# Five mixing products placed in three parts of a streaming encoder layer on one core

## What is computed

```python
z = rms_norm(x, g_mix) @ w_in
q_lat, c_kv, k_r, u, v = split(z)
# group A: latent attention, 8 heads, for prompt and for sample
q = norm_rope(rms_norm(q_lat) @ w_q_up)
k, v_att = norm(c_kv_all @ w_kv_up)        # sample: 1024 cached rows + 64 new
o_att = softmax(q k / sqrt(96)) v_att
# group B: spatial gating, 8 groups of 64 columns, chunks of 128 positions
vn = layer_norm(gelu(v))
mixed = einsum('gij,bcjgd->bcigd', masked(w_s), vn) + b_s
o_gm = gelu(u) * mixed
x = x + concat(rms_norm(o_att), rms_norm(o_gm)) @ w_o
x = x + (silu(h @ w_gate) * (h @ w_up)) @ w_down     # h = rms_norm(x)
```

## Time and profile before

| | |
|---|---|
| median of 3 runs | 1410.85 us |
| lowest and highest | 1410.61 and 1413.23 us |
| time of the profiled execution | 1417.39 us |
| its span, first to last instruction | 1415.6 us |
| mean granted TensorE clock | 0.981 |
| PE busy | 1352.3 us (96%) |
| DVE, ACT, POOL busy | 912.7, 599.5, 866.3 us |

### The profile page before, as it was taken

One profiled execution on the slowest core, in us unless ns is written; L12 is line 12 of the kernel. 1 busy time (PEld: TensorE's weight loads), 2 busy tenths in 40 slices (PEclk: granted clock), 3 DMA queues, 4 the chain that ended last, 5 costly groups with the idle time before them and its releaser, 6 DMA issues.

```text
span 1415.6 us, 25340 instructions
## 1 busy us (share of the span) xinstructions
PE 1352.3 (96%) x9448; PEld 1247.7 (88%) x9448; DVE 912.7 (64%) x1490; ACT 599.5 (42%) x953; POOL 866.3 (61%) x460
## 2 busy tenths in 40 slices
PE   6999989998999999999999989889899999999998
PEld 6885657898999999999998756779899999999997
DVE  3456467487666766676736475665866766666665
ACT  4336467444333333333342365764443333333331
POOL 3645057286777777777655443464777777777771
PEclk8999999999999999999999999999999999999999
DMA  7110021131322222222421000221232222222221
GB/s 229 60 38 11 5 61 30 32 89 54 96 90 89 89 89 89 89 89 89 130 89 52 26 5 1 60 60 31 60 90 90 89 89 89 89 89 89 89 89 68
DMA packets 138577, 102.35 MB, mean 72 GB/s; under 512 B 8972, under 2 KB 125136, under 8 KB 138512
## 3 DMA queue, kind: packets, MB, share of 16 engines
q1 hardware_dynamic: 135848, 100.46, 23.6%
q10 hardware_dynamic: 2664, 1.02, 0.3%
HBM read 98.10 MB, written 3.36 MB: 72 GB/s over the span
## 4 chain that ended last, share of the span: by engine, by line
PE 83%; DVE 9%; ACT 2%; issue 2%; POOL 2%; DMA 1%; ACTq 0%; SPq 0%; DVEq 0%
PE ps L2199 33%; PE ps L1907 9%; PE ps L1911 9%; PE ps L1908 9%; PE ps L1852 4%; PE ps L1890 3%; PE ps L1891 3%; PE ps L1892 3%; PE ps L2140 2%; PE ps L2120 2%; POOL rs L754 2%; PE ps L2004 2%; PE ps L2010 1%; DVE hs_lo L1312 1%; PE ps L2097 1%
## 5 line engine op out<-in xcount | busy, mean ns | idle before, releaser
L754 POOL TENSOR_TENSOR rs<-ms,mhalf 128x8 f32<-128x8 f32 (+5 forms) x66 | 139.7, 2120 | 200.8 <-DVE ms L1442 80.5
L853 POOL TENSOR_TENSOR w_lo<-raw,w_hi 128x1024 fp32r<-128x1024 f32 x132 | 229.9, 1769 | 42.4 <-ACT w_hi L1263 39.7
L1677 DVE TENSOR_REDUCE raw<-raw 128x512 f32<-128x1024 f32 x184 | 230.6, 1254 | 0.5
L853 POOL TENSOR_TENSOR w_lo_a<-raw,w_hi_a 128x512 fp32r<-128x512 f32 x88 | 179.5, 2052 | 69.8 <-ACT w_hi_a L1263 69.8
L1907 PE MATMUL ps<-act_hi,w_hi 128*128 128x288 f32 x704 | 195.9, 293 | 3.5 <-issue 3.5
L1908 PE MATMUL ps<-act_lo,w_hi 128*128 128x288 f32 x704 | 196.1, 294 | 0.0
L1639 DVE TENSOR_TENSOR xT<-ps,xT 128x576 f32<-128x576 f32 x192 | 142.3, 751 | 46.3 <-PE ps L1911 46.2
L2199 PE MATMUL ps<-t_hi,w_hi 128*128 128x288 f32 x528 | 157.4, 298 | 7.4 <-DVE side L1702 6.1
L2199 PE MATMUL ps<-t_lo,w_hi 128*128 128x288 f32 x528 | 156.8, 297 | 0.0
L2199 PE MATMUL ps<-t_hi,w_lo 128*128 128x288 f32 x528 | 156.5, 296 | 0.0
L1911 PE MATMUL ps<-act_hi,w_lo 128*128 128x288 f32 x704 | 150.5, 295 | 0.0
(11 more groups left out here) (239 smaller groups left out, 3496.9 us busy)
## 6 DMA issues: line engine op xcount, KB each, us to landing
raw<-in_w_gate SPq DMA_DIRECT2D x88, 256.0 KB, 3.7
raw<-in_w_up SPq DMA_DIRECT2D x88, 256.0 KB, 3.6
raw<-in_w_down SPq DMA_DIRECT2D x20, 1024.0 KB, 4.9
raw<-in_w_in SPq DMA_DIRECT2D x10, 1024.0 KB, 5.5
raw<-in_w_o SPq DMA_DIRECT2D x16, 512.0 KB, 5.3
x_tm<-in_x_prompt SPq DMA_DIRECT2D x4, 512.0 KB, 5.2
raw<-in_w_down SPq DMA_DIRECT2D x8, 256.0 KB, 3.5
out_y_prompt<-x_tm SPq DMA_DIRECT2D x8, 256.0 KB, 2.2
```

The costliest lines, as they stand in the source:

```text
L754: pool.tensor_tensor(rs[:, c:c + n], ms[:, c:c + n], mhalf[:, 0:n], ALU.pow).then_inc(rs_ready, 1)
L853: pool.tensor_tensor(lo[:, k, cols], src, hi[:, k, cols].bitcast(F32), ALU.subtract).then_inc(lo_split, 1)
L1677: dve.tensor_reduce(raw[:, 2, j * Q:(j + 1) * Q], added(a, b), AX.X, ALU.add).then_inc(sums_added, 1)
```

## The change

Mixing units 0 and 1 go behind sample prep step 9 on PE, ahead of step 10 (which turns tile 8). Unit 2 goes behind step 11, which turns tile 9. Units 3 and 4 go behind the scores of the first sample step. DVE takes units 0 to 2 where it took all five, and units 3 and 4 behind the minima of the first sample step. The plan lists the banks in PE's order. ACT, POOL and SP have the same code as before.

```diff
+MIXES = [(0, 1), (2,), (3, 4)]
...
-        prep(L["s_preps"], S_TILES, range(1, len(S_TILES) + 2))
-        L["mix"] = [ring.add("mix_out") for _ in range(5)]
+        L["mix"] = []
+
+        def mix(tiles):
+            L["mix"] += [ring.add("mix_out") for _ in tiles]
+
+        prep(L["s_preps"], S_TILES, range(1, len(S_TILES)))
+        mix(MIXES[0])
+        prep(L["s_preps"], S_TILES, range(len(S_TILES), len(S_TILES) + 2))
+        mix(MIXES[1])
...
                 steps[n]["s"] = [ring.add("s_exp") for _ in S_SPANS]
+            if n == 0:
+                mix(MIXES[2])
...
 # DVE
-                for g2 in range(4):
...
+                def mix_taken(g2):
...
+                for g2 in MIXES[0] + MIXES[1]:
+                    mix_taken(g2)
 
                 dve.wait_ge(v_stored, 16 * (l + 1))
                 for n in range(HEAD_PAIRS + 2):
...
                         dve.tensor_reduce(nm[:, n % 4, 0:1], mx[:, 4 * (n % 2):4 * (n % 2) + 3], AX.X, ALU.min).then_inc(nm_ready, 1)
+                    if n == 0:
+                        for g2 in MIXES[2]:
+                            mix_taken(g2)
...
 # PE
-                preps_run(L["s_preps"], range(1, len(S_TILES) + 2))
...
+                def mix(g2):
...
+                preps_run(L["s_preps"], range(1, len(S_TILES)))
                 pe.wait_ge(vn_done, l + 1)
                 pe.wait_ge(wsT_masked, l + 1)
                 emptied(pe, L["u"][-1])
+                for g2 in MIXES[0]:
+                    mix(g2)
+                preps_run(L["s_preps"], range(len(S_TILES), len(S_TILES) + 2))
+                for g2 in MIXES[1]:
+                    mix(g2)
 
                 emptied(pe, L["s_preps"][-1]["turn"][0])
...
                             ins.then_inc(full, 1)
+                    if n == 0:
+                        for g2 in MIXES[2]:
+                            mix(g2)
                     if 1 <= n <= HEAD_PAIRS:
```

More of the change, by code:

```diff
@@ L1504, in _ @@
                 preps_run(L["s_preps"], range(1, len(S_TILES) + 2), v_affine)
-                for g2 in range(4):
+                def mix_taken(g2):
                     u = L["mix"][g2]
                     filled(dve, u)
[L1510 to L1515, removed]
-                    ins.then_inc(S["mix_out"], 1)
@@ L1517, in _ @@
[L1517 to L1525, removed]
+                    if g2 < 4:
+                        for e in range(2):
+                            g = 2 * g2 + e
+                            dst = ug[:, 0:PT_, g * GDIM:(g + 1) * GDIM]
+                            ins = dve.scalar_tensor_tensor(
+                                out=dst, in0=ps[:, u.bank, e * 256:(e + 1) * 256].rearrange("p (t d) -> p t d", t=PT_),
+                                scalar=gT[:, G_BS + GROUPS * l + g:G_BS + GROUPS * l + g + 1], in1=dst,
+                                op0=ALU.add, op1=ALU.mult)
+                    else:
+                        for g in range(GROUPS):
+                            dst = ug[DEC:P, PT_, g * GDIM:(g + 1) * GDIM]
+                            ins = dve.scalar_tensor_tensor(
+                                out=dst, in0=ps[DEC:P, u.bank, g * GDIM:(g + 1) * GDIM],
+                                scalar=gT[DEC:P, G_BS_S + GROUPS * l + g:G_BS_S + GROUPS * l + g + 1], in1=dst,
+                                op0=ALU.add, op1=ALU.mult)
@@ L2041, in _ @@
                 emptied(pe, L["ct"][3])
-                preps_run(L["s_preps"], range(1, len(S_TILES) + 2))
+                def mix(g2):
+                    u = L["mix"][g2]
+                    free(u)
+                    if g2 < 4:
+                        for e in range(2):
+                            g = 2 * g2 + e
+                            ins = pe.matmul(ps[:, u.bank, e * 256:(e + 1) * 256].rearrange("p (t d) -> p t d", t=PT_),
+                                            wsT[:, g, :], gv[:, 0:PT_, g * GDIM:(g + 1) * GDIM], start=True, stop=True)
+                    else:
+                        for g in range(GROUPS):
+                            ins = pe.matmul(ps[DEC:P, u.bank, g * GDIM:(g + 1) * GDIM], wsT_s[DEC:P, g, :],
+                                            gv[DEC:P, PT_, g * GDIM:(g + 1) * GDIM], start=True, stop=True)
+                    ins.then_inc(full, 1)
+                preps_run(L["s_preps"], range(1, len(S_TILES)))
                 pe.wait_ge(vn_done, l + 1)
```

## The result

The changed kernel takes 1410.05 us (median of 20 executions, 1400.31 to 1411.35) against 1413.36 us for the kernel before (20 executions, 1407.22 to 1422.70). The ratio is **0.9958, with a 95% interval of 0.9941 to 0.9976**: faster by 0.42%. The direction was right, the size about twice too large, and the time lies outside the range.

The account below looks back on a forecast made before the run. PE's work, gaps and clock were taken as the bound. A 6.0 us gain a layer, less 0.3, gave 11.4 us for two layers, off the 1410.85 us median: 1399.5 us. The range was 1396.0 to 1406.3 us.

Parts of the forecast that it names:

- the turns of exponentials: PE's first two turns of exponentials in layer 0's sample attention: to start 6.1 and 6.0 us earlier.
- one gap of 0.79 us ahead of turn 9: PE's gaps of 1.18 and 1.14 us ahead of turns 8 and 9 were to become one of 0.6 us.
- DVE's first minimum bound by the stored rows of gv: After the first sample scores, DVE was to wait for the gv transfer, issued at 141.4 and landing at 143.6 us.
- the second exponentials: ACT's second exponentials in the sample attention: to end at 151.45 us, with PE waiting 0.1 us at most.
- One price: A mixing unit on PE at full clock: taken as 0.95 us, between bounds of 0.86 and 1.03 us.
- the 0.3 us taken off: Allowance per layer for hops between engines and banks coming just in time, lowering 6.0 to 5.7 us.
- Sum: 6.0 us a layer: Gain per layer from the layer 0 schedule, with everything from the values' product on moving as a block.
- the clock was not low in the unprofiled runs: Rival, chance 0.17: unprofiled mixing and turn 9 already at full clock; gain 2.8 us a layer, time 1405.3 us.
- both layers show the same fall: Argument against the rival of unprofiled runs without low clock: PE's clock fell alike at mixing in both profiled layers.
- rival of a cold sample attention: Rival, chance 0.02: units 3 and 4 make PE wait between first scores and last values' product; up to 1419.5 us.
- The clock falls all the same: Rival, chance 0.18: PE still at half clock from 140.45 to 147.25 us; gain 3.1 us a layer, time 1404.6 us.
- later gaps that give back what was won: Case, chance 0.03: the sum holds, but later gaps, moved by 6 us, return nearly all; no change.

Follow-up runs that it names:

- quiet versions: Changed kernel and kernel before, each with unused products filling PE's gaps at prompt step 15 and ahead of the output projection: 1399.1 and 1405.7 us.
- look1: The kernel before, unedited, run again for one more trace of its mixing stage; means of the three such runs 1412.8 to 1414.7 us.
- look2: The kernel before, unedited, the second of three such further traces; means of the three 1412.8 to 1414.7 us.
- look3: The kernel before, unedited, the third of three such further traces; means of the three 1412.8 to 1414.7 us.
- the fill: Two unused products in PE's gap at prompt step 15, against the same kernel without them: 1400.1 us on the changed kernel, 1406.2 us on before.
- rep_before: The kernel before, unedited, run once more for a second trace: 1413.5 +- 1.3 us, ratio 0.9996.

## Why the prediction was wrong

**The schedule was right.** The trace after agrees within 0.3 us with the steps that carry the sum: the turns of exponentials at 148.11 and 151.43 (148.25 and 151.45 forecast), one gap of 0.79 us ahead of turn 9 (0.6), DVE's first minimum bound by the stored rows of gv (143.32; 143.6), the second exponentials ending in time for PE to wait no more than a moment. One price was half a us off and cost nothing: units 0 and 1 took 0.86 us each, the lower bound, not 0.95, and turn 8 started at 138.54 for 139.05. The gain in the first trace was 5.9 us a layer for 6.0 (5.7 with the 0.3 us taken off).

**The step that failed is "Sum: 6.0 us a layer", as a statement on every execution.** It is two terms of different kinds. One is the gaps and the overlap: the measure goes from 20.1 us in a warm layer of before to 17.4 us, 2.7 us a layer, 5.3 us in all (unrounded 2.66). It is 17.4 us in all ten traced layers with the full change, and the timed executions bear it out: 5.2 +- 0.3 us at equal low clock. The other is the clock: 23.3 less 20.1 is 3.2 us a layer, 6.5 us in all, and it was read off one execution in which both layers happened to be cold for the full 6.8 us. Measured were 5.8 +- 0.8 us between the kernels as they are, and 6.6 +- 1.1 us between their quiet versions: the first term, and little or nothing of the second. In the terms of the clock, the forecast took 13.6 us at low clock away (6.8 us in each layer), and 1.4 +- 1.7 us went (50.3 to 48.9 us), worth 0.5 us at 0.38 us each.

The rival "the clock was not low in the unprofiled runs" (0.17) is nearest to what happened. Its gain of 5.6 us is the measured one, in part by luck: its condition, a clock that never falls at mixing, held in four of ten traced layers only. It was given too little because "both layers show the same fall" was taken for a rule of the kernel. It was one execution: look1, look2 and look3 have 3.4 and 0, 0 and 3.4, 0 and 0 us there. The hint in the numbers (the profiled execution 6.5 us above the median) pointed the right way, though half of it was the low median of the three runs. By the ten layers the clock term should have been carried at half of its size, not whole.

**The base was off as well.** The median of the three runs, 1410.85 us, is 3.4 us under the mean of 138 executions, 1414.3 us. 1399.5 + 3.4 for the base + 5.6 for the gain that didn't come (11.4 - 5.8) is 1408.5 us, the measured mean. That the three runs lay low was chance; no working from one trace could have shown it.

**The range** took in 1406.3 us. It had the right rival, but on the low base; that rival on the mean of before stands at 1408.7 us.

The rival of a cold sample attention did not happen: no trace after has low clock there. "The clock falls all the same" did not either, in any of the traced layers with units 0 and 1 early. The last one, later gaps that give back what was won, is what the first trace after shows in layer 0; over all executions the order's gain stayed, and only the clock's was not there.

What stays open: ten traced layers of before lose 1.6 us each on the mean to cold mixing ((4 x 3.2 + 2 x 1.6)/10), so that 3 us in all should come back with warm mixing, and 0.0 +- 1.1 and -1.0 +- 1.9 us did. In time at low clock, before without its cold mixing would have 50.3 - 6.8 = 43.5 us, and the changed kernel has 48.9 +- 1.5. Behind the gap in the prompt attention, four traced layers of the changed kernel have 12 us at low clock on the mean and ten of before 5 us, but the equal worth of the fill on both speaks against a lasting difference there. Either the ten layers were colder than the usual, or a shifted stage changes how later gaps meet the clock, as the first trace after suggests. No run here tells these apart.

## What to carry to other kernels

A price read at half clock is a price of that execution. Split the gain into what the order of the work gives in every execution, taken between two warm layers, and what the clock gives, and weigh the second by how often the stage is cold in several traces. Where single executions of one kernel differ by more than the change is worth (here 1400 to 1417 us for the changed kernel), three runs don't fix the base either; the granted clock beside each time takes most of that scatter out. In this kernel, filling a gap of the matrix engine ahead of short products with unused ones was worth more (8 us) than moving useful work: the changed kernel with two fills a layer took 1399.1 us, 1.1% below before.

## What was not expected of the hardware

Half clock can outlast full work by far. In the prompt attention, PE was busy for 8.00 of 8.00 and 6.00 of 6.00 us at a clock of 0.50, for 17.1 us in all, behind a gap of 1.51 us. In the unedited kernel before the same gap was followed by 17.1 us of it (look3), by 3.4 us (first trace, rep_before) and by none (look1). Behind the kernel's start, low stretches came in lengths of 3.4, 6.8 and 17.1 us (once 20.5). And the same code with the same gaps was cold in one execution and warm in the next. The Trainium skill (TensorE: Matmul & The Clock Gate, Part 4: PE-mode transpose) says that transposes don't count for the full clock as matmuls do. In the changed kernel two turns in a row, 0.79 us apart, did not lower the clock in any trace (1.9 us of mixing stood ahead of them), so here the rule did not decide; its share in the 17 us stretch, where turns, scores and short products alternate, was not tested.
